# First stage of a one-core decoder layer in two token halves, with the second x tiles loaded later

## The reference

```
ada = silu(c) @ w_ada + b_ada                     # (1, 6*1024): shift1, scale1, gate1, shift2, scale2, gate2
h = rms_norm(x, norm1_g) * (1 + scale1) + shift1  # rms over the 1024 channels of a token
proj = h @ w_in                                   # 1024 -> 2816 columns
```

## Time and profile before

| | |
|---|---|
| median of 3 runs | 1123.74 us (1121.43 to 1123.8) |
| the profiled execution | 1120.4 us |
| its span, first to last instruction | 1118.6 us |
| PE busy | 1082.1 us, 97% of the span |
| DVE busy | 779.3 us, 70% |
| ACT busy | 443.5 us, 40% |
| POOL busy | 250.4 us, 22% |
| DMA | 161.16 MB, mean 144 GB/s |
| mean granted TensorE clock | 0.995 |

### The profile page before, as it was taken

How to read it: one execution, slowest core, us unless ns; L and a number is a source line. 1 busy time by engine, 2 the same in 40 slices (tenths; PEclk the granted TensorE clock), 3 DMA queues, 4 the chain that set the end, 5 groups by cost and what they waited for, 6 DMA issues and landing times. The chain is left out here.

```text
span 1118.6 us, 14165 instructions
## 1 busy us (share of the span) xinstructions
PE 1082.1 (97%) x5210; PEld 877.3 (78%) x5210; DVE 779.3 (70%) x1214; ACT 443.5 (40%) x754; POOL 250.4 (22%) x219
## 2 busy tenths in 40 slices
PE   5999999999999999988999999999899999999998
PEld 4678877777778898766788888888777888888886
DVE  5673556565546777789978787878886866957852
ACT  6342334445444334573332323333523423515331
POOL 2011000000001114404232323222231423223331
PEclk9999999999999999999999999999999999999999
DMA  9958333333013104012654545356916744446305
GB/s 280 277 167 264 123 119 103 119 103 115 25 43 110 34 20 126 7 57 87 198 193 147 186 145 194 133 198 207 349 55 226 263 145 143 168 148 232 107 1 151
DMA packets 155509, 161.16 MB, mean 144 GB/s; under 512 B 14852, under 2 KB 125616, under 8 KB 152368
## 3 DMA queue, kind: packets, MB, share of 16 engines
q1 hardware_dynamic: 147376, 131.89, 36.3%
q0 software_dynamic: 8064, 28.36, 7.8%
HBM read 117.75 MB, written 42.47 MB: 143 GB/s over the span
## 5 line engine op out<-in xcount | busy, mean ns | idle before, releaser
L801 PE MATMUL ps<-cmb_hi,wm_hi 128*128 128x512 f32 x880 | 345.2, 392 | 15.6 <-DVE cmb_lo L2064 5.0
L803 PE MATMUL ps<-cmb_hi,wm_lo 128*128 128x512 f32 x880 | 342.6, 389 | 0.0
L802 PE MATMUL ps<-cmb_lo,wm_hi 128*128 128x512 f32 x880 | 342.5, 389 | 0.0
L801 PEld LDWEIGHTS ps<-cmb_hi,wm_hi 128*128 128x128 f32 x880 | 165.2, 188 | 55.4 <-DVE x1t L2260 9.2
L803 PEld LDWEIGHTS ps<-cmb_hi,wm_lo 128*128 128x128 f32 x880 | 165.2, 188 | 34.6
L802 PEld LDWEIGHTS ps<-cmb_lo,wm_hi 128*128 128x128 f32 x880 | 165.3, 188 | 33.9 <-issue 0.2
L801 PE MATMUL ps<-act_hi,w_hi 128*128 128x512 f32 x400 | 162.4, 406 | 3.0 <-DVE act_lo L1767 3.0
L802 PE MATMUL ps<-act_lo,w_hi 128*128 128x512 f32 x400 | 156.9, 392 | 0.0
L803 PE MATMUL ps<-act_hi,w_lo 128*128 128x512 f32 x400 | 156.9, 392 | 0.0
L1457 ACT ACTIVATE wm_hi<-wm_f 128x512 fp32r<-128x512 f32 x128 | 77.2, 627 | 184.7 <-POOL wm_f L771 138.1
L2260 DVE SCALAR_TENSOR_TENSOR x1t<-ps,ada,x1t 128x512 f32<-128x512 f32 x112 | 83.5, 745 | 76.0 <-PE ps L803 76.0
(11 more groups left out here) (208 smaller groups left out, 1435.8 us busy)
## 6 DMA issues: line engine op xcount, KB each, us to landing
raw<-in_w_mlp_dram SPq DMA_DIRECT2D x128, 256.0 KB, 3.9
wada<-in_w_ada_dram POOLq DMA_DIRECT2D x32, 512.0 KB, 4.9
h_spill<-stage SPq DMA_DIRECT2D x32, 512.0 KB, 5.8
cmb_f<-h_spill SPq DMA_DIRECT2D x10, 1024.0 KB, 7.1
w_raw<-in_w_in_dram SPq DMA_DIRECT2D x18, 512.0 KB, 3.9
ada_rows<-in_w_ada_dram SPq DMA_DIRECT2D x16, 512.0 KB, 7.2
cmb_f<-h_spill SPq DMA_DIRECT2D x16, 512.0 KB, 7.1
h_spill<-stage SPq DMA_DIRECT2D x24, 256.0 KB, 4.8
```

What stands on the lines that cost most here:

```text
L801: pe.matmul(bank, wh, hi, start=first, stop=False, skip_group_check=onto)
L802: pe.matmul(bank, wh, lo, start=False, stop=False, skip_group_check=onto)
L803: return pe.matmul(bank, wl, hi, start=False, stop=last, skip_group_check=onto)
```

## The change

The first stage goes by token halves. SP loads x tiles 0 to 3, then w_ada rows 0, w_in tiles 0 and 1, w_ada rows 1, and only then x tiles 4 to 7, then rows 2 and on. Once tiles 0 to 3 are turned, their inverse rms is spread and the first half of k-tiles 0 and 1 is modulated and multiplied, with the turns of tiles 4 to 7 between. Then the second half of k-tiles 0 and 1, then k-tiles 2 to 7 by both halves. Tiles 4 to 7 are all turned through banks 1 and 3 (those of the second half's products), each after the copy of the one before; the second spread goes to bank 1; an x tile is copied in two pieces, one for each bank; the squares have a buffer of their own, as ht1 is used at the same time. The semaphores count products of the new order (`MODULATED`).

```diff
+MODULATED = [(0, 0), (1, 0), (0, 1), (1, 1)] + [(_k, _h) for _k in range(2, KT) for _h in range(2)]
+        def n_mod(k, half):
+            return MODULATED.index((k, half)) + 1
-        sqj = at("sqj", [2, D], TMPB + 4 * KB)
+        sqj = at("sqj", [2, D], REG + 80 * KB)
 # SP
-            for n in range(NB):
+            def load_x(n):
...
+            for n in range(XS):
+                load_x(n)
...
                 if t == 1:
-                    for k in range(1, KT - 1):
+                    load_rows(1)
+                    for n in range(XS, NB):
+                        load_x(n)
+                    for k in range(2, KT - 1):
                         load_rows(k)
 # PE
             def rms_spread(half):
                 pe.wait_ge(s_diag, half + 1)
-                pe.matmul(ps[:, 6 + half, :], ...
+                if half:
+                    pe.wait_ge(s_xt, NB)
+                pe.matmul(ps[:, (6, 1)[half], :], ...
+            def x_turn(n):
                 pe.wait_ge(s_xin[n], 16)
-                wait(pe, s_xt, n - 1)
+                wait(pe, s_xt, n - 1 if n < XS else n)
                 for k in range(KT):
-                    tr = pe.transpose(ps[:, 2 * (n % 2) + k // 4, tokens(k % 4)], xin[:, n % XS, tokens(k)], ident)
+                    bank = 2 * (n % 2) + k // 4 if n < XS else 1 + 2 * (k // 4)
+                    tr = pe.transpose(ps[:, bank, tokens(k % 4)], xin[:, n % XS, tokens(k)], ident)
                 tr.then_inc(s_xtp, 1)
+            def first_product(t, k, half):
+                if k < 2:
+                    pe.wait_ge(s_wlo if k else s_wk, t + 1)
+                pe.wait_ge(s_act1, n_mod(k, half))
+                mm = passes(ps[:, 2 * t + half, :], ...)
+            for n in range(XS):
+                x_turn(n)
+            pe.wait_ge(s_vrow, 16 * 8)
+            pe.transpose(ps[:, 5, 0:V_ROWS], vrow[...], ...).then_inc(s_vt, 1)
             ada_sums(0)
+            rms_spread(0)
             ada_columns(0)
-            (for each k: t = 0 by both halves, sums of k + 2, t = 1 by both halves, columns of k + 2;
-             sums 1, columns 1, sums 2 and columns 2 with k-tile 0)
+            pe.wait_ge(s_xt, XS)
+            first_product(0, 0, 0)
+            x_turn(4)
+            first_product(1, 0, 0)
+            ada_sums(1)
+            x_turn(5)
+            ada_columns(1)
+            x_turn(6)
+            first_product(0, 1, 0)
+            first_product(1, 1, 0)
+            x_turn(7)
+            rms_spread(1)
+            ada_sums(2)
+            pe.wait_ge(s_rbc, 2)
+            first_product(0, 0, 1)
+            first_product(1, 0, 1)
+            ada_columns(2)
+            ada_sums(3)
+            first_product(0, 1, 1)
+            first_product(1, 1, 1)
+            ada_columns(3)
+            for k in range(2, KT):
+                (as before for each k)
 # ACT: after the squares of tiles 0 to 3, rms_sd(0) and vec
+            ada_copy(0)
+            rms_copy(0)
+            split_next(-1)
+            modulated_hi(0, 0)
+            split_next(0)
+            x_square(4)
+            ada_copy(1)
+            x_square(5)
+            modulated_hi(1, 0)
+            x_square(6)
+            x_square(7)
+            rms_sd(1)
+            rms_copy(1)
+            modulated_hi(0, 1)
             ada_copy(2)
-            for k in range(1, KT - 1):
-                modulated_hi(k + 1)
+            modulated_hi(1, 1)
+            ada_copy(3)
+            for k in range(2, KT):
+                modulated_hi(k, 0)
+                modulated_hi(k, 1)
                 if k + 2 < KT:
                     ada_copy(k + 2)
 # DVE
+            def x_copy(n):
                 dve.wait_ge(s_xtp, n + 1)
-                dve.tensor_copy(xt[:, :, tokens(n)], bank_pair(n % 2)...)
+                for b in range(2):
+                    bank = 2 * (n % 2) + b if n < XS else 1 + 2 * b
+                    copy = dve.tensor_copy(xt[:, b * HK:(b + 1) * HK, tokens(n)], ps[:, bank, :]...)
+                copy.then_inc(s_xt, 1)
+            for n in range(XS):
+                x_copy(n)
+            rms_diag(0)
...
+            modulation(0)
+            scaled(0, 0)
+            first_lo(0, slice(0, 1)).then_inc(s_wk, 1)
+            modulated_lo(0, 0)
+            first_lo(1, slice(0, 1)).then_inc(s_wk, 1)
+            x_copy(4)
+            first_lo(0, slice(1, KT)).then_inc(s_wlo, 1)
+            first_lo(1, slice(1, KT)).then_inc(s_wlo, 1)
+            x_copy(5)
+            modulation(1)
+            scaled(1, 0)
+            x_copy(6)
+            modulated_lo(1, 0)
+            x_copy(7)
+            rms_diag(1)
             dve.wait_ge(s_xt, NB)
+            scaled(0, 1)
+            scaled(1, 1)
+            modulated_lo(0, 1)
+            modulated_lo(1, 1)
+            for k in range(2, KT):
+                (modulation, scaled and modulated_lo by both halves, as before)
```

More of the change, by code:

```diff
@@ L924, in attend @@
                 mm.then_inc(s_pv, 1)
+            def first_product(t, k, half):
+                if k < 2:
+                    pe.wait_ge(s_wlo if k else s_wk, t + 1)
+                pe.wait_ge(s_act1, n_mod(k, half))
+                mm = passes(ps[:, 2 * t + half, :], w_hi[:, t, k, :], w_lo[:, t, k, :], act_hi[:, k, HALVES[half]],
+                            act_lo[:, k, HALVES[half]], k == 0, k == KT - 1)
+                if (k, half) == (KT - 1, 1):
+                    mm.then_inc(s_mmp, 1)
@@ L928, in _ @@
+            for n in range(XS):
+                x_turn(n)
+            pe.wait_ge(s_vrow, 16 * 8)
+            pe.transpose(ps[:, 5, 0:V_ROWS], vrow[0:V_ROWS, :], cst[0:V_ROWS, C_ID:C_ID + V_ROWS]).then_inc(s_vt, 1)
             ada_sums(0)
+            rms_spread(0)
             ada_columns(0)
[L930 to L952, removed]
@@ L954, in _ @@
+            ada_sums(3)
[3 more added lines that the diff above has]
+            for k in range(2, KT):
+                first_product(0, k, 0)
+                first_product(0, k, 1)
+                if k + 2 < KT:
+                    ada_sums(k + 2)
+                first_product(1, k, 0)
+                first_product(1, k, 1)
+                if k + 2 < KT:
+                    ada_columns(k + 2)
             for t in range(2, N_PROJ):
@@ L1278, in rms_copy @@
                 act.wait_ge(s_rbp, half + 1)
-                act.activation(rbc[:, HALVES[half]], ps[:, 6 + half, :], ACT.Copy).then_inc(s_rbc, 1)
+                act.activation(rbc[:, HALVES[half]], ps[:, (6, 1)[half], :], ACT.Copy).then_inc(s_rbc, 1)
             def ada_copy(k):
@@ L1284, in ada_copy, with modulated_hi, x_square @@
                 act.activation(asb[:, k % 2, :], ps[:, 4 + k % 2, 0:2 * P], ACT.Copy).then_inc(s_asb, 1)
[L1286 to L1292, removed]
+            def modulated_hi(k, half):
+                act.wait_ge(s_t1, n_mod(k, half))
+                act.activation(act_hi[:, k, HALVES[half]], ht1[:, k % 2, HALVES[half]], ACT.Identity,
+                               bias=ada[:, k:k + 1]).then_inc(s_hi1, 1)
+            def x_square(n):
                 act.wait_ge(s_xin[n], 16)
@@ L1759, in scaled, with modulated_lo @@
                     dve.wait_ge(s_rbc, half + 1)
-                wait(dve, s_act1, 2 * (k - 2) + half + 1)
+                if k >= 2:
+                    dve.wait_ge(s_act1, n_mod(k - 2, half))
                 dve.scalar_tensor_tensor(out=ht1[:, k % 2, HALVES[half]], in0=xt[:, k, HALVES[half]], scalar=a1[:, k:k + 1],
                                          in1=rbc[:, HALVES[half]], op0=ALU.mult, op1=ALU.mult).then_inc(s_t1, 1)
[L1764 to L1767, removed]
-                                             scalar=ada[:, k:k + 1], in1=act_hi[:, k, HALVES[half]].bitcast(F32),
-                                             op0=ALU.add, op1=ALU.subtract).then_inc(s_act1, 1)
+            def modulated_lo(k, half):
+                dve.wait_ge(s_hi1, n_mod(k, half))
+                dve.scalar_tensor_tensor(out=act_lo[:, k, HALVES[half]], in0=ht1[:, k % 2, HALVES[half]],
+                                         scalar=ada[:, k:k + 1], in1=act_hi[:, k, HALVES[half]].bitcast(F32),
+                                         op0=ALU.add, op1=ALU.subtract).then_inc(s_act1, 1)
             def first_lo(t, ks):
```

49 lines of the change are left out of this document (13 added, 36 removed).

## The result

In 12 runs of each, the changed kernel takes 1132.76 us in the median (1127.23 to 1135.99), the kernel before 1122.72 (1117.99 to 1126.89). The ratio is 1.0081, with a 95% interval from 1.0064 to 1.0098: **9.1 us slower** (7.2 to 11.0). The forecast was +6.6. The profiled execution has a span of 1129.6 us, 11.0 more than before.

The account below looks back on a forecast made before the run. PE is busy 97% of the span and idles only ahead of tile 2, so the change shifts tile 2's start: 3.7 + 1.5 + 1.4 = +6.6 us on 1123.7, giving 1130.3 us, range 1125.8 to 1134.6.

Parts of the forecast that it names:

- case (a): The forecast as summed, with one fall of the clock in the head: 1130.3 us, own range 1128 to 1132; chance 0.50.
- case (b): Clock falls again or stays at half until k-tile 2: +3.8 us on the forecast, 1134.1 us; chance 0.18.
- Landings: SP's queue after x tile 3: rows 0 at 13.4 us, rows 1 at 20.6, x tiles 4 to 7 from 21.9 to 25.9.
- The first product: Head of the kernel: first product starts at 19.9 us instead of 26.61, 6.7 us won but not kept.
- First term: First product to k-tile 2: turns, copies and modulation wait in one written order; k-tile 2 at 45.45 against 41.76, +3.7 us.
- Second term: Loop over k-tiles 2 to 7: ACT's changed order makes rounds 4.72 us against 4.42, and a longer last step; +1.5 us.
- Third term: Head: the clock falls to half in PE's new lull and is back at 26.1 us; +1.4 us, bounds 0 and 2.7.
- its two grounds: For (b), 31.1 to 42.6 us: PE works some 6 of 11 us; by the skill page, turns would not hold the clock.
- (c): No fall of the clock at all: +5.2 us, 1128.9 us; chance 0.18.
- (d): Faster: tile 7's landing alone sets the end of the head, no loss in the loop; -3.1 us, 1120.6 us; chance 0.06.
- (e): Within 0.2%: turn 7 at 27 to 30 us and no clock fall, say +1 us, 1124.7 us; chance 0.08.
- the signs named ahead: New profile: turn 7 near 32.7, four 1.3 us copies, PE stops of some 2 us, 0.3 us pause per round, rest unchanged.

Follow-up runs that it names:

- after_warm2: Changed kernel with 52 filler matmuls (identity times identity, result unread) cut to PE's lulls in the first stage: 1126.58 us, 1.0028 of the kernel before.
- order_only: Changed kernel with SP's loads in the old queue order, all x tiles first: 1140.15 us, 1.0158 of the kernel before.
- turn7_warm: after_warm2 with the turn of tile 7 ahead of k-tile 1's products and two filler strings cut from 8 to 4: 1122.25 us, 0.9993 of the kernel before.
- before_warm2: Kernel before with 11 filler matmuls after the first columns and 7 before the columns of k-tile 2: 1118.38 us, 0.9955 of the kernel before.
- loads_only: Kernel before with only the order of SP's loads changed to the new one; PE, ACT and DVE as before: 1133.86 us, 1.0101 of the kernel before.
- act_warm: after_warm2 with ACT's old order in the loop, act_hi of k + 1 ahead of the copy of sums k + 2: 1126.6 us, 1.0024 of the kernel before.
- before_turns2: Kernel before with transposes of the identity as fillers in its two lulls, 19 and 12: 1119.29 us, 0.9975 of the kernel before.
- new_best: Changed kernel with fillers, turn 7 ahead of k-tile 1's products and ACT's old order in the rounds: 1121.09 us, 0.9989 of the kernel before.
- before_warm: Kernel before with 16 filler matmuls ahead of its first product, none in the second lull: 1120.62 us, 0.9975 of the kernel before.

## Why the prediction was right, and where its size was off

The sign, the mechanism of hand-overs and most of the size came out as forecast: 9.1 us (7.2 to 11.0) against 6.6, and the time of 1132.76 lies in the range but outside case (a)'s own (1128 to 1132), nearer to case (b)'s 1134.1. The path that the clock took is not that of case (a), which had 0.50, but that of case (b), which had 0.18; so the number came nearer to the forecast than its account of the clock deserved.

**Landings: right in kind, about 1 to 2 us early.** Rows 0 were awaited until 15.33, not 13.4: the rows that follow x tile 3 at 9 to 11 us move at 133 to 154 GB/s, which no row of before showed. Tile 4 was squared on ACT as it landed, at 23.7 in the changed kernel and 22.9 in after_warm2, not at 21.9.

**The first product: 23.41, not 19.9.** 1.9 us of it is the landing of rows 0. The other 1.6 is the clock, which fell at the end of that wait, at 15.6: the sums took 1.75 instead of 1.07 and the spread 2.08 instead of 1.12. I had looked for the fall only behind the spread. The wait for rows 0 ahead of it was 3.54 us of idle PE, from 11.8 on; my landing time made it 1.6.

**First term (+3.7, the written order): right.** With the clock held, k-tile 2 starts at 45.77 where the sum said 45.45, through the same chain of waits: turn 6 for copy 5, k-tile 1's products for the act_lo behind copy 6, turn 7 behind the products, the spread, the second half. Tile 4 was 1.1 later than summed, the rest 0.7 shorter. order_only shows that the arrival of the tiles is not what makes the stretch long in this order, and turn7_warm that 1.9 us of it is the one turn's place. Against before_warm2 the term is 5.1, since the kernel before had paid 1.1 to its own clock. How much of it the later loads would cost at full clock without the new order of work, no run shows: loads_only and order_only had no fillers. The split copy took 1.29 (1.30 in the sum).

**Second term (+1.5, the loop): right mechanism, 0.9 measured.** Rounds take 4.57 and not 4.72, so four of them cost 0.6, and k-tile 6 to 7 takes 3.26 and not 3.35, 0.35 more than before. act_warm removes it whole.

**Third term (+1.4, the clock): mis-sized.** It priced one fall. The profile has four stretches at 0.50, and with them tile 2 stands 6.7 us behind after_warm2 (76.85 against 70.17); in the kernel before the clock cost 1.1 (65.28 against 64.19). Net 5.6. Up to 0.8 of the 6.7 may not be the clock's: rows 0 and tile 4 landed 0.6 and 0.8 later in the changed kernel's profile than in after_warm2's. In the profiles the sum reads 5.1 + 0.9 + 5.6 = 11.6 for the 11.57 measured; that it adds up is no proof, as all three are differences between the same four profiles. That is what case (b) described, and its 3.8 on top of the 1.4 is near. Of its two grounds one stands (PE idle for much of the stretch) and one is out. By the Trainium skill's page "TensorE: Matmul & The Clock Gate", Part 4, turns would not keep the clock up. before_turns2 shows that they do here (clock 1.00 from 8 to 65 us with 31 turns as the only fill). What lets the clock fall is the stops of PE at the hand-overs, not the kind of its work: with them filled the clock stayed, by matmuls in both kernels and by turns in the kernel before, and where new_best left one open ahead of turn 4 (1.33 us) it fell.

**What stays open.** The medians share the loss out otherwise. With the clock held on both sides the ratio is 1.0028 / 0.9955 = 1.0073, 8.2 us (5.5 to 11), and fillers win 0.53% (3 to 9 us) on the changed kernel and 0.45% (3.4 to 6.9 us) on the one before: a net share of the clock of about 1 us (up to 4 by the intervals), where single profiles give 5.6. The granted clocks of the timed runs settle a part of this. The profiled execution of the kernel before had 0.995, better than each of the 73 runs set beside the experiments (0.986 to 0.994), so its profile shows too little of what the clock costs it. The clock knows two levels here, so twice what it lacks to 1, times the span, is the time at half. By this estimate the kernel before spent 22 us at half clock in the mean of those 73 runs and 11.5 with fillers (before_warm2), the changed kernel 33.5 and 14.2 (after_warm2). So fillers took away 10 to 12 us of half clock from the one and 19 from the other, 7 to 9 us apart, where the heads of the two profiles are 13.7 apart (20.5 and 6.8). At what the fillers won for each such microsecond (0.3 to 0.5) that is a net share of some 2 to 4 us, which the medians allow and the 5.6 isn't. The two further looks at the kernel before agree (10.2 us at half clock in the head). The rest isn't settled: from tile 2 to the end one profile differs from another by up to 5.5 us, and two profiles can't be set against two medians to better than that. That the order of loads and work, at full clock, costs half of the loss or more holds by both accounts (6.0 of 11.6 us in the profiles, 8.2 of 9.1 in the medians); how the rest divides doesn't.

**The rivals.** (c), no fall, is out by the windows. (d), tile 7's landing sets the end, is out by turn 7 starting at 37.38 behind the products and by order_only. (e), +1 us, is out by the interval. Of the signs named ahead, the four separate copies, the stops of some 2 us (2.13, 2.19 and 1.60), k-tile 2 after 45 and the unchanged rest came as told. The times of turn 7 and of the spread's end (32.7 and 37 in the forecast) were 37.38 and 42.6, and came out only with the clock held (33.38 and 37.7). The first product by 21 did not come, and the pause was 0.15 us a round, not 0.3.

## What to carry to other kernels

Here a first product 3.2 us earlier was worth nothing, because the halves' turns, copies and modulations were then written into one order across three engines. Count the hand-overs between the first product and the first full round, not the time of the first product. A turn that something long hangs on belongs ahead of products that nothing waits for. Where PE must stand idle at such hand-overs, matmuls into an unread PSUM range, cut to end before the operand is ready, were worth 0.45% on the kernel before. before_warm, whose string ended late and which left the second lull open, won 0.25%; the intervals overlap, and whether the late string or the open lull cost anything isn't shown. One profile of a kernel can be a lucky one: set its granted clock beside those of the timed runs before a share of the loss is read from it.

## What the hardware showed that I hadn't expected

- Turns of fp32 tiles hold the clock as matmuls do: 31 of them in two lulls kept it at 1.00 from 8 to 65 us, and at a mean of 0.992 to 0.997 in 12 runs.
- A string of 16 fillers was 32 records and 3.82 us; 19 transposes of the same size were 19 records and 2.27 us. An fp32 matmul of 128 columns costs two records here, a turn one.
- The spread of runs on the changed kernel narrows with fillers: 8.8 us between the lowest and the highest of 12 without, 3.0 in 10 runs of after_warm2, 5.0 to 5.9 in 10 to 12 runs of the four other kernels with fillers made from it. On the kernel before it is less clear (3.4 in 6 runs with matmuls, 8.8 in 12 with turns, 8.9 in 12 without).
- The DMA's rate dips to 107 to 212 GB/s for 2 us where w_ada rows follow x tile 3, in all seven profiles with that order, and then settles near 290, against 397 for x alone; where the same rows follow x tile 7 at 16 to 18 us it doesn't dip.
